# All eight value pages of a sample in one visit, and jobs on part of the array side by side

## The reference

```
x = x_prompt (1, 512, 1024)  and  x_sample (8, 1, 1024)
z = rmsnorm(x) @ w_in                      # q, k, v of 8 heads x 64, q, k, v, o of 4 mLSTM heads x 128, gates
# samples: past keys and values through the page table, 8 pages of 128 tokens, 8 heads x 64
k_past = cache_k[page_table];  v_past = cache_v[page_table]
s      = q . k / 8, only the chosen blocks of 256 tokens and the own token
attn   = softmax(s) @ v                    # the part that the change moves: P = softmax weights, times the value pages
# mLSTM in parallel, its own state per sample
x = x + concat(attn, mlstm) @ w_out
x = x + square(relu(rmsnorm(x) @ w_up)) @ w_down
y = rmsnorm(x)
```

## Time and profile before

| | us |
|---|---|
| median of 3 runs | 701.5 |
| the profiled execution, its own time | 702.04 |
| its span | 700.3 |
| TensorE busy | 686.1 |
| VectorE busy | 445.8 |
| ScalarE busy | 296.4 |
| GpSimd busy | 323.4 |
| the 64 value pages: first and last start of their matmuls | 172.0 to 274.9 |

### The profile page before, as it was taken

One profiled execution on the slowest core, in us unless ns is written; L12 is line 12 of the kernel. 1 busy time (PEld: TensorE's weight loads), 2 busy tenths in 40 slices (PEclk: granted clock), 3 DMA queues, 4 the chain that ended last, 5 costly groups with the idle time before them and its releaser, 6 DMA issues.

```text
span 700.3 us, 15196 instructions
## 1 busy us (share of the span) xinstructions
PE 686.1 (98%) x5563; PEld 641.2 (92%) x5563; DVE 445.8 (64%) x890; ACT 296.4 (42%) x568; POOL 323.4 (46%) x233
## 2 busy tenths in 40 slices
PE   6999999999999999999999999999999999999996
PEld 6999988878777777999999999999999999999996
DVE  4388899886342446537788695857657576575134
ACT  6532735465342233146555444443433534334222
POOL 6829999823131434247327607053260623507431
PEclk9999999999999999999999999999999999999999
DMA  7944999944486887633102313332232332413103
GB/s 245 301 118 150 291 285 265 271 141 113 140 253 202 256 270 182 134 117 122 61 25 98 121 61 123 120 104 81 86 125 86 120 96 66 141 62 121 61 1 123
DMA packets 88633, 100.41 MB, mean 143 GB/s; under 512 B 5374, under 2 KB 64338, under 8 KB 88570
## 3 DMA queue, kind: packets, MB, share of 16 engines
q1 hardware_dynamic: 74566, 92.91, 42.5%
q10 hardware_dynamic: 14004, 6.67, 4.0%
HBM read 92.92 MB, written 6.64 MB: 142 GB/s over the span
## 4 chain that ended last, share of the span: by engine, by line
PE 87%; DVE 7%; ACT 2%; issue 2%; POOL 1%; DMA 1%; DVEq 0%; POOLq 0%; ACTq 0%
PE acc L915 9%; PE acc L916 8%; PE acc L917 8%; PE acc L1419 5%; PE acc L1418 5%; PE acc L1420 5%; PE scr L1419 3%; PE scr L1420 3%; PE scr L1418 3%; PE scr L1385 3%; PE scr L1384 3%; PE scr L1386 3%; PE acc L1384 3%; PE acc L1386 3%; PE acc L1385 3%; PE acc L1206 2%
## 5 line engine op out<-in xcount | busy, mean ns | idle before, releaser
L915 PE MATMUL acc<-act_hi,w_hi 128*128 128x256 f32 (+1 forms) x416 | 121.8, 293 | 0.5 <-DVE zT L2504 0.5
L2020 POOL TENSOR_TENSOR h_lo<-relu,h_hi 128x520 fp32r<-128x520 f32 x32 | 44.1, 1382 | 165.0 <-ACT h_hi L1805 164.7
L916 PE MATMUL acc<-act_lo,w_hi 128*128 128x256 f32 (+1 forms) x416 | 117.3, 282 | 0.0
L917 PE MATMUL acc<-act_hi,w_lo 128*128 128x256 f32 (+1 forms) x416 | 117.2, 282 | 0.0
L1504 POOL TENSOR_TENSOR w_lo<-raw,w_hi 128x1024 fp32r<-128x1024 f32 x24 | 57.2, 2390 | 96.8 <-ACT w_hi L1497 94.5
L1973 POOL TENSOR_TENSOR prod<-kv,Qb 128x1024 f32<-128x1024 f32 x32 | 85.8, 2714 | 16.3 <-DVE S L2206 10.4
L915 PEld LDWEIGHTS acc<-act_hi,w_hi 128*128 128x128 f32 x416 | 78.4, 188 | 6.1 <-issue 4.9
L916 PEld LDWEIGHTS acc<-act_lo,w_hi 128*128 128x128 f32 x416 | 78.5, 189 | 0.0
L917 PEld LDWEIGHTS acc<-act_hi,w_lo 128*128 128x128 f32 x416 | 78.2, 188 | 0.0
L2523 DVE TENSOR_TENSOR xT<-acc,xT 128x260 f32<-128x260 f32 x64 | 26.6, 424 | 48.4 <-PE acc L1420 48.4
L2504 DVE TENSOR_TENSOR zT<-acc,rstd 128x264 f32<-128x264 f32 (+1 forms) x56 | 23.5, 421 | 46.0 <-PE acc L917 42.2
(11 more groups left out here) (422 smaller groups left out, 2303.9 us busy)
## 6 DMA issues: line engine op xcount, KB each, us to landing
kv<-in_cache_k_dram SPq DMA_DIRECT2D x64, 256.0 KB, 3.5
kv<-in_cache_v_dram SPq DMA_DIRECT2D x64, 256.0 KB, 3.0
raw<-in_w_up_dram SPq DMA_DIRECT2D x16, 1024.0 KB, 5.4
raw_d<-in_w_down_dram SPq DMA_DIRECT2D x12, 1024.0 KB, 5.1
raw<-in_w_in_dram SPq DMA_DIRECT2D x14, 512.0 KB, 6.0
raw<-in_w_in_dram SPq DMA_DIRECT2D x7, 1024.0 KB, 7.0
x_tok<-in_x_prompt_dram SPq DMA_DIRECT2D x8, 512.0 KB, 5.4
raw<-in_w_out_dram SPq DMA_DIRECT2D x4, 1024.0 KB, 6.6
```

The lines of the kernel that those rows point to most:

```text
L915: pe.matmul(out, W_HI[home(g)][:, k, :], hi[k][:, cols], start=(n == 0), stop=False)
L916: pe.matmul(out, W_HI[home(g)][:, k, :], lo[k][:, cols], start=False, stop=False)
L917: mm = pe.matmul(out, W_LO[home(g)][:, k, :], hi[k][:, cols], start=False, stop=(n == KT - 1))
L2020: pool.tensor_tensor(h_lo[:, t, :], relu2[:, t % 2, :], h_hi[:, t, :].bitcast(F32), ALU.subtract).then_inc(s_hs_lo, 1)
```

## The change

In `plan()`, both visits of a sample are put in the later slot, `pv_slot(b) + 1`. Then the tasks of each slot that holds a `pv` are sorted: all others first in their old order, then those that work on part of the array, in the order att_s, pv, sm_r, att_o, pv_pick, pv_mask, mix_att. The list of loads is not touched. Because two names of a sample stand next to each other, its eight matmuls do as well.

```diff
     for b in range(NS):
         for r in range(2):
-            at(pv_slot(b) + r, ("pv", b, r))
+            at(pv_slot(b) + 1, ("pv", b, r))
         if b < 4:
             at(pv_slot(b) + 2, ("s_put", b + 4))
...
     for t in range(4):
         at(ATT[t] + 8, ("att_o", t), ("mix_att", t))
+    tiled = "att_s", "pv", "sm_r", "att_o", "pv_pick", "pv_mask", "mix_att"
+    for names in tasks:
+        if any(name[0] == "pv" for name in names):
+            names.sort(key=lambda name: (name[0] in tiled, tiled.index(name[0]) if name[0] in tiled else 0))
```

## The result

| | before | after |
|---|---|---|
| median, us | 701.71 (14 runs) | 703.15 (14 runs) |
| lowest to highest | 701.22 to 702.36 | 701.04 to 705.99 |
| the profiled execution, its own time | 702.04 | 703.90 |
| its span | 700.3 | 702.2 |

The ratio after to before is 1.0023 (1.0016 to 1.0030). The kernel became slower by 0.2%. The forecast was 701.2 us with a range up to 703.1, so the time lies just outside it and the sign of the likeliest case was wrong. The profiled execution of the change is 0.75 us above the median, so its stalls are a little larger than those of a middle run.

What follows compares the result with a forecast made beforehand. TensorE, busy 98% of the span, was taken as the bound. Median 701.5, less 1.96 for its stream, plus 1.35 and 0.1 for late pages and 0.2 for a bank, gave 701.2 us; range 699.7 to 703.1.

Steps and rivals of the forecast that it cites:

- the likeliest case: Whole kernel: 701.2 us, slightly faster than 701.5, with own bounds 700.2 to 702.6; chance 0.58.
- TensorE's stream: Value stage: joined visits and new neighbours on TensorE save 1.96 us, bounds 1.5 and 2.3.
- The fourth sample's pages: Fourth sample's visit, end of slot 44: pages wanted at 11.2, there at 12.4 us; costs 1.35, bounds 1.1 and 1.6.
- The other intervals: Remaining gaps between visits: five last 12.4 us or longer and cost nothing if a page lands in 2.9.
- 0.1 for the sixth sample: Fifth to sixth visit, slots 46 to 48: 11.7 us, just over the limit; costs 0.1, bounds 0 and 0.5.
- Pages late at more visits: Rival: last pages of the sixth or seventh sample also land late, up to 704.0 us; slower, chance 0.15.
- the one line on later stages: Sign against the forecast: wrong in kind if a later stage gives back or takes more than 0.3 us.
- The bank of `C_stage`: Slot 52: sm_r(2) waits for the PSUM bank that DVE empties; up to 0.85 us, taken as 0.2.
- The boundaries don't exist as reckoned: Rival: order makes no difference on TensorE but joining does; +0.8, 702.3 us, counted as same; chance 0.07.
- the pages come in time: Rival: no visit waits for pages, so the gain stands alone at 699.7 us; faster, chance 0.20.
- The range: Whole kernel, 8 in 10: 699.7 to 703.1 us, from the middle of the fast case into the nearer slow one.

Runs made afterwards that it cites:

- the change with both edits: The changed kernel with SyncE reading a sample's eight page numbers ahead and n_prompt written after the output's first three phases: 699.18 us, 699.50 in the last group.
- the page numbers ahead: The changed kernel, but SyncE reads a sample's eight page numbers before it waits for the first free page: 700.34 us, 2.8 below the change.
- the later writing of n_prompt: The changed kernel, but ScalarE's n_prompt column is written after the first three phases of the output: 702.36 us, 0.8 below the change.
- joining alone: The kernel before with a sample's eight pages in one visit, no sorting: 704.51 us; 701.09 with page numbers read ahead and n_prompt written late.
- sorting alone: The kernel before with part-array jobs sorted to the slot's end, visits of four: 700.67 us; 700.60 with page numbers ahead and n_prompt late.

## Why the prediction was wrong, point by point

The forecast was 701.5 - 1.96 + 1.35 + 0.1 + 0.2 = 701.2. Against it stands 701.7 - 2.4 + 2.8 + 0.8 to 1.1 = about 703.1, in which 2.4 is the change with both edits, 2.8 what the page numbers ahead give back, and 0.8 to 1.1 what the later writing of n_prompt gives back (without and with the other edit). The forecast had put 1.45 where 2.8 stands, and nothing where 0.8 to 1.1 stands.

- **TensorE's stream: right in kind, too small.** -1.96 was forecast, -2.42 read from the trace with the stalls taken out, -2.36 measured. Slot by slot the forecast held to 0.1 us. The largest misses are in slot 53 (+0.57 instead of +0.67), 44 (+0.88 instead of +0.96) and 38 (+0.73 instead of +0.79); the visit itself is 1.85 to 1.86, not 1.88, and sm_r follows at 1.74, not 1.76. In most slots a few hundredths are missing in the same direction; why, no run shows. Summed this is 0.46 us, just past the bound of -2.3.
- **The fourth sample's pages: right.** 1.35 was forecast and 1.55 measured. (The wait inside it was given as 1.25; its own terms give 12.39 - 11.19 = 1.20.) The interval was reckoned at 10.3 and is 10.34 from start to start (205.85 to 216.19). The rest is that the eight issues took 8.41 us instead of 8.05.
- **The other intervals: this step failed.** "The other five intervals are 12.4 us or longer by the same reckoning and cost nothing if a page lands in 2.9", and 0.1 for the sixth sample. The need was reckoned at 11.5 us, so the forecast had some 0.9 us to spare at the seventh visit and 0.2 at the sixth. The intervals came out as reckoned, 12.41 (244.65 to 257.06) and 11.74 (232.91 to 244.65). Two other terms were mis-sized. The eight issues took 0.94 longer (8.99 instead of 8.05), though the text called their distance regular, and the last page landed in 4.9 instead of 2.9: 0.94 + 2.0 - 0.9 is 2.0, and 2.08 was lost there. In another profile it was the sixth sample, with regular issues and a landing of 4.7: 1.8 - 0.2 is 1.6, and 1.65 was lost. The spare time was compared with the landing's median, 2.9, and not with its longest.
- **The rival that named this mechanism was right in its mechanism.** "Pages late at more visits" had 704.0 with a chance of 0.15. Its point of decision for the seventh sample was a landing over 3.9 us. It took its longer landings from the earlier trace rows, where a weight block stands in front. Here the weight blocks did come behind, as the text said; at the seventh sample the landings go with state writes on ScalarE's queue, and at the sixth their cause is open. (Its sum takes 1.6 as the smallest gain where the bound was given as 1.5; that is 0.1 us.)
- **The held-up copy: this step failed too.** About 1 us, with no term and no rival: the write of n_prompt and the DMA engines behind it don't occur in the forecast. The reckoning ended with the value stage, and the one line on later stages ("gives back or takes more than 0.3 us") is where it would have shown.
- **The bank of `C_stage`: 0 instead of 0.2.** The forecast moved TensorE and left VectorE's copy nearly where it was. With the sorting the copy comes 1.06 us earlier behind the product (1.65 instead of 2.71), and the wait is gone; with joining alone it is 0.8, the forecast's "up to 0.85".
- **"The boundaries don't exist as reckoned" and "the pages come in time"** fell: sorting alone gives 1.26 us with both edits (1.17 in the stretch), and the pages are late.
- **The range.** The bounds of the unknown costs were added around the likeliest case alone. With 1.65 to 2.08 us for one more late visit, on the forecast of 701.2, it would have reached 702.9 to 703.3, and with the held-up copy further.

## What to carry to other kernels

When buffers that came free at two times come free at one, reckon the refill per interval: first issue, number of issues times their distance, and the longest landing, not the median, against the time until the last one is wanted. Here 0.9 us to spare was not enough: 2.1 us were lost in one profile and nothing in others. And before joining uses, make the refill itself fast: here, reading the table entries ahead turned a loss of 0.2% into a gain of 0.3 to 0.4% together with one small write moved.

## What the runs showed of the hardware that was not expected

- Between two page issues of SyncE 1.10 us lie when the page number is read from memory in between, and 0.52 when the eight are read ahead (4.24 us for eight). At 0.52 the landing grows from 2.9 to as much as 6.5 us, so the last page comes only 0.9 us earlier (217.7 instead of 218.6), though its issue comes 4.5 us earlier.
- A page of 256 KB can land late while the DMA engines have almost nothing else to do: 4.7 us after its issue, with 17 GB/s moved in its last 2 us.
- A write of 512 pieces of 4 bytes on ScalarE's queue is followed by five or more microseconds with under 75 GB/s in all seven profiles that have it in this place, down to 46 packets in 4 us (5 GB/s) in the change; the seven profiles with the write moved have no such stretch. With it VectorE starts a copy some 2 us late in three of the seven profiles. Without it, the runs above 703 us of sorting alone are gone. In the kernel before the same stretch costs nothing.
- Stalls inside a row of sixteen matmuls of one line don't always appear as idle time of the matmuls: 1.55 us at the fourth visit stood in the distance between starts, and in the rows of the weight loads.
